# A norm between two projections, cut into halves of the tokens and put between the products of its neighbours

## The reference

```python
    y = merged @ w_out[l]
    x = x + gate * _rms(y, g_post[l])
...
    hn = rms_norm(h, norm_mixer[i])        # h is that x
...
    proj = h @ w_in                        # q, k, v, g, a_lr of the GLA mixer
    log_a = log_sigmoid(a_lr @ w_a2 + b_a) / 16
```

## Time and profile before

| | |
|---|---|
| median of three runs | 2327.85 us |
| the profiled execution | 2328.21 us |
| its span, first to last instruction | 2326.0 us |
| TensorE busy | 2200.5 us (95%) |
| VectorE busy | 1205.2 us (52%) |
| ScalarE busy | 856.5 us (37%) |
| GpSimd busy | 554.3 us (24%) |
| TensorE's mean granted clock | 0.975 |

### The profile page before, as it was taken

How to read it: one execution, slowest core, us unless ns; L and a number is a source line. 1 busy time by engine, 2 the same in 40 slices (tenths; PEclk the granted TensorE clock), 3 DMA queues, 4 the chain that set the end, 5 groups by cost and what they waited for, 6 DMA issues and landing times.

```text
span 2326.0 us, 29165 instructions
## 1 busy us (share of the span) xinstructions
PE 2200.5 (95%) x11168; PEld 1853.8 (80%) x11168; DVE 1205.2 (52%) x1488; ACT 856.5 (37%) x1295; POOL 554.3 (24%) x292
## 2 busy tenths in 40 slices
PE   4999999999999699999899979999999999999996
PEld 4778888988887598898778868888888888877885
DVE  6963332543331724334345454566666667676744
ACT  3136653112021323323322123446546546544311
POOL 1322221333333122222233222211111111111520
PEclk9999999999999699999999989999999999999998
DMA  8112222112331211101131121111111011012201
GB/s 338 53 46 73 73 72 73 55 37 89 137 136 46 82 36 46 37 28 46 36 138 44 46 99 56 37 46 36 45 54 43 29 54 45 27 45 101 81 19 73
DMA packets 36660, 154.59 MB, mean 66 GB/s; under 512 B 4161, under 2 KB 4161, under 8 KB 35810
## 3 DMA queue, kind: packets, MB, share of 16 engines
q1 hardware_dynamic: 23840, 93.52, 11.6%
q10 hardware_dynamic: 12738, 59.87, 7.2%
HBM read 128.15 MB, written 21.04 MB: 64 GB/s over the span
## 4 chain that ended last, share of the span: by engine, by line
PE 83%; DVE 11%; issue 4%; ACT 2%; DMA 0%; DVEq 0%; SPq 0%; ACTq 0%
PE psG L311 21%; PE psG L312 21%; PE psG L313 21%; PE psA L311 3%; PE psA L313 2%; PE psA L312 2%; PE psA L1884 1%; PE psA L1883 1%; PE psA L1858 1%; PE psA L1784 1%; DVE M L871 1%; PE psA L399 1%; DVE AL L824 1%; DVE AL L849 1%; PE psA L1867 1%
## 5 line engine op out<-in xcount | busy, mean ns | idle before, releaser
L311 PE MATMUL psG<-AH,WH 128*128 128x512 f32 x2108 | 856.8, 406 | 40.3 <-DVE AL L849 15.3
L312 PE MATMUL psG<-AL,WH 128*128 128x512 f32 x2108 | 831.8, 395 | 0.0
L313 PE MATMUL psG<-AH,WL 128*128 128x512 f32 x2108 | 830.8, 394 | 0.0
L298 POOL TENSOR_SCALAR WH<-RAW 128x1024 fp32r<-128x1024 f32 x144 | 165.3, 1148 | 1685.3 <-PE psG L311 1195.7
L311 PEld LDWEIGHTS psG<-AH,WH 128*128 128x128 f32 x2108 | 401.7, 191 | 124.7 <-issue 28.0
L313 PEld LDWEIGHTS psG<-AH,WL 128*128 128x128 f32 x2108 | 401.3, 190 | 88.1
L312 PEld LDWEIGHTS psG<-AL,WH 128*128 128x128 f32 x2108 | 402.9, 191 | 69.5
L300 POOL TENSOR_TENSOR WL<-RAW,WH 128x1024 fp32r<-128x1024 f32 x144 | 389.2, 2703 | 12.0
L2183 DVE TENSOR_TENSOR FTL<-PF,FTH 128x512 fp32r<-128x512 f32 x192 | 112.8, 588 | 129.2 <-ACT FTH L2058 127.2
L2051 ACT ACTIVATE PF<-psA,PB 128x512 f32<-128x512 f32 x192 | 111.3, 580 | 91.6 <-PE psA L1886 52.1
L2193 DVE RECIPROCAL FDR<-psA 64x128 f32<-64x128 f32 x128 | 118.2, 939 | 32.1 <-PE psA L313 30.5
(11 more groups left out here) (331 smaller groups left out, 2961.3 us busy)
## 6 DMA issues: line engine op xcount, KB each, us to landing
RAW<-w_tiles SPq DMA_DIRECT2D x144, 512.0 KB, 3.5
gates<-SIG ACTq DMA_DIRECT2D x16, 512.0 KB, 2.9
park<-X ACTq DMA_DIRECT2D x2, 4096.0 KB, 11.1
CB<-fox_c ACTq DMA_DIRECT2D x16, 512.0 KB, 4.3
X<-xT SPq DMA_DIRECT2D x4, 1024.0 KB, 11.9
WADA_SCALE<-w_ada SPq DMA_DIRECT2D x1, 4096.0 KB, 24.0
WADA_SHIFT<-w_ada SPq DMA_DIRECT2D x1, 4096.0 KB, 34.0
WADA_GATE<-w_ada ACTq DMA_DIRECT2D x1, 4096.0 KB, 16.4
```

The costliest lines, as they stand in the source:

```text
L298: nc.gpsimd.tensor_scalar(WH[:, i, :], RAW[:, i % RAW_SLOTS, :], 1.0, 0.0, ALU.mult, ALU.add).then_inc(w_high, 1)
L311: first = nc.tensor.matmul(out, wh, xh, start=start, stop=False)
L312: nc.tensor.matmul(out, wh, xl, start=False, stop=False)
L313: return first, nc.tensor.matmul(out, wl, xh, start=False, stop=stop)
```

## The change

**Output projection of block 1** (`pe_block1_out`). Tiles 0 to 3 are computed as before. Tiles 4 to 7 are computed first for the low 512 tokens (LO), into the four banks of `psG`, then for the high 512 (HI) into the same banks. Between the slices of the HI products TensorE does the half sum and half spread of the first norm, and eight half sums of the squares of the updated x, one for each chunk, into columns of their own of `psA`, which VectorE adds up (`tensor_reduce`). VectorE updates x for LO in this time, with PSUM banks 1 and 3 of `psA` for its products.

**The next tiles** (`pe_gla_begin`). LR and q are computed for LO, chunk by chunk, q two chunks behind LR; between them the sum and spread of the first norm for HI. Then k for LO with a half sum of the HI squares behind each of its eight slices; the spread; LR and q for HI; the logits of head 0; k for HI. The cumulated decay follows behind k now, where it stood before k. k goes to `psA` and q and the logits change units (`gla_buf`).

ScalarE's and VectorE's lists follow with twice as many instructions of 512 columns; the parking of x (a DMA of 4 MB) is issued behind the HI updates.

**Weighted sums** (`weigh`). Of the three matmuls of a piece the one with `FTL` is now the third and only it waits for `ft_ready`; the first two wait for `ft_high`.

```diff
+    def pe_block1_out(pe):
+        for j in range(WHOLE):
+            gemm(pe, T_WO + j, U_WO + j, (T_WO + j) % 4, (U_WO + j) % 2, fill=2 if j == 0 else None)
+        for j in range(WHOLE, KC):
+            pe.wait_ge(w_split, T_WO + j + 1)
...
+            for c in range(KC):
+                f, l = half_cut(psG[:, j - WHOLE, :], (T_WO + j) % 4, c, LO)
...
+            l.then_inc(wo_full, 1)
+        for j in range(WHOLE, KC):
+            pe.wait_ge(wo_free, j - WHOLE + 1)
+            for c in range(KC):
+                f, l = half_cut(psG[:, j - WHOLE, :], (T_WO + j) % 4, c, HI)
+                if j > WHOLE and c == 0:
+                    f.then_inc(tile_begun, 1)
+                if (j, c) == (WHOLE, 2):
+                    pe.wait_ge(lo_added, KC - WHOLE)
+                    pe_half_sums(RS, 0, 0)[1].then_inc(lo_sums, 1)
+                elif (j, c) == (WHOLE, 4):
+                    pe.wait_ge(lo_rec, 1)
+                    pe_half_spread(0).then_inc(lo_spread, 1)
+                elif (j - WHOLE) * KC + c in LO_SUMS_AT:
+                    pe_lo_squares(LO_SUMS_AT.index((j - WHOLE) * KC + c))
+            l.then_inc(psum_full, 1)
+        pe.wait_ge(lo_rec, 2)
+        pe_half_spread(0).then_inc(lo_spread, 1)
+
+    def pe_gla_begin(pe):
+
+        lag, q = 2, T_GLA % 4
+        for n in range(KC + lag):
+            if n < KC:
...
+                pe.wait_ge(lo_ready, n + 1)
+                f, l = half_cut(psG[:, 0, :], T_LR % 4, n, LO)
...
+            if n >= lag:
...
+                half_cut(psG[:, 2, :], q, n - lag, LO)
+            if n == 0:
+                pe.wait_ge(sq_used, sq_base(2))
+                pe_half_sums(RS, 1, 8)[1].then_inc(sum_full, 1)
+            elif n == 3:
+                pe.wait_ge(rc_ready, 2)
+                pe_half_spread(1).then_inc(rs_full, 1)
+        pe.wait_ge(w_split, T_GLA + 2)
+        for j in range(KC):
+            half_cut(psA[:, 3, :], (T_GLA + 1) % 4, j, LO)
+            pe.wait_ge(sq_ready, KC * SPLIT_NORM + j + 1)
+            third, l = pe_half_sums(SQ[:, j % 2, :], 1, 16 + 4 * j)
...
+        pe.wait_ge(rc_ready, 3)
+        pe_half_spread(1).then_inc(rs_full, 1)
+        for n in range(KC + lag):
+            if n < KC:
+                pe.wait_ge(a_ready, KC * 3 + n + 1)
+                _, l = half_cut(psG[:, 1, :], T_LR % 4, n, HI)
...
+            if n >= lag:
+                f, l = half_cut(psG[:, 3, :], q, n - lag, HI)
...
+        pe.wait_ge(wa_loaded, 32)
+        pe.wait_ge(psum_free, U_LR + 1)
+        pe_gla_logits(pe, 0)
+        for c in range(KC):
+            f, l = half_cut(psA[:, 2, :], (T_GLA + 1) % 4, c, HI)
...
     def dve_block1_out(dve):
...
+        def update(j, cols, spread, done):
+
+            if j >= 2:
+                dve.wait_ge(done, j - 1)
+
+            rows_ = psA[:, 1 + 2 * (j % 2), :] if cols == LO else TN[:, j % 2, cols]
+            link(nc.vector.scalar_tensor_tensor(rows_, Y[:, j, cols], GG[:, j:j + 1], spread, ALU.mult, ALU.mult))
+            nc.vector.tensor_tensor(X[:, j, cols], X[:, j, cols], rows_, ALU.add).then_inc(done, 1)
...
+        for j in range(KC + 1):
+            fill(j, LO, lo, (0, 0), lo_tn, lo_high, lo_ready)
+            if j == 2:
+                dve.wait_ge(rms_ready, 2)
+                nc.vector.reciprocal(RC[:, 4:8], RC[:, 4:8]).then_inc(rc_ready, 1)
         dve.wait_ge(rs_full, 2)
         for j in range(KC):
...
+            update(j, HI, hi, x_upd)
+        dve_gla_in(dve)
+        dve.wait_ge(sum_full, 3)
...
             r, h, n, lo, w = piece(j)
-            pe.wait_ge(ft_ready, p * N_P + (j + 1))
+            pe.wait_ge(ft_high, p * N_P + (j + 1))
...
             vs = slice(HD * r, HD * r + P)
-            _, l = three(psA[:, 2 + r, HALF - w:HALF], FVH[:, n, vs], FVL[:, n, vs], FTH[:, j % 2, 0:w], FTL[:, j % 2, 0:w],
-                         n == 0, j in ENDS)
-            l.then_inc(fpv_done, 1)
+            out = psA[:, 2 + r, HALF - w:HALF]
+            nc.tensor.matmul(out, FVH[:, n, vs], FTH[:, j % 2, 0:w], start=n == 0, stop=False)
+            nc.tensor.matmul(out, FVL[:, n, vs], FTH[:, j % 2, 0:w], start=False, stop=False)
+            pe.wait_ge(ft_ready, p * N_P + (j + 1))
+            nc.tensor.matmul(out, FVH[:, n, vs], FTL[:, j % 2, 0:w], start=False, stop=j in ENDS).then_inc(fpv_done, 1)
```

More of the change, by code:

```diff
@@ L400, in pe_sums, with pe_half_sums @@
         return l
[L402 to L408, removed]
+    LO, HI = slice(0, HALF), slice(HALF, S)
+    WHOLE = KC // 2
+    def pe_half_sums(src, h, at):
+        for n in range(NB // 2):
+            s = (NB // 2 * h + n) * P
+            l = nc.tensor.matmul(psA[:, 2, at + n:at + n + 1], src[:, s:s + P], mat("ones")[:, 0:1], start=True, stop=True)
+            if n < NB // 2 - 1:
+                third = l
+        return third, l
@@ new lines, in build, with pe_lo_squares, pe_half_spread, half_cut @@
+    LO_SUMS_AT = [12, 14, 17, 19, 22, 24, 27, 29]
+    def pe_lo_squares(j):
+        pe = nc.tensor
+        pe.wait_ge(lo_squares, KC - WHOLE + j + 1)
+        pe_half_sums(SQL[:, j % 2, :], 0, 48 + 4 * j)[1].then_inc(lo_taken, 1)
+    def pe_half_spread(h):
+        for n in range(NB // 2):
+            m = NB // 2 * h + n
+            l = nc.tensor.transpose(psA[:, h, n * P:(n + 1) * P], RC[:, m:m + 1].to_broadcast([P, P]), mat("ident"))
+        return l
+    def half_cut(out, slot, c, cols):
+        ws = slice(c * P, (c + 1) * P)
+        return three(out, WH[:, slot, ws], WL[:, slot, ws], AH[:, c, cols], AL[:, c, cols], c == 0, c == KC - 1)
@@ new lines, in copy_hi, with fill_lo @@
+        def copy_hi(j):
+            nc.scalar.activation(Y[:, j, HI], psG[:, j - WHOLE, :], ACT.Copy).then_inc(psum_free, 1)
+        behind = {0: 4, 2: 5, 5: 6}
+        for j in range(KC):
+            updated(j)
+            if j in behind:
+                square_hi(behind[j])
+                copy_hi(behind[j])
+        square_hi(KC - 1)
+        act.wait_ge(sum_added, 1)
+        act_half_root(0, RC[:, 0:4]).then_inc(lo_root, 1)
+        copy_hi(KC - 1)
+        def fill_lo(j):
+            act.wait_ge(lo_tn, j + 1)
+            nc.scalar.activation(AH[:, j, LO], TN[:, j % 2, LO], ACT.Copy).then_inc(lo_high, 1)
@@ L775, in build @@
+        for j in range(KC):
+            act.wait_ge(tn_ready, KC + j + 1)
+            nc.scalar.activation(AH[:, j, HI], TN[:, j % 2, HI], ACT.Copy).then_inc(a_high, 1)
     chain = Chain(nc.vector, dve_step)
@@ new lines, in fill, with low @@
+        def fill(j, cols, spread, base, tn, high, ready):
+            def low(j):
+                dve.wait_ge(high, base[1] + j + 1)
+                nc.vector.tensor_tensor(AL[:, j, cols], TN[:, j % 2, cols], AH[:, j, cols].bitcast(F32), ALU.subtract).then_inc(ready, 1)
+            if j < KC:
+                if j >= 2:
+                    dve.wait_ge(ready, base[1] + j - 1)
+                nc.vector.scalar_tensor_tensor(TN[:, j % 2, cols], X[:, j, cols], col("norm0", j), spread, ALU.mult, ALU.mult).then_inc(tn, 1)
+            if j:
+                dve.wait_ge(tn, base[0] + j)
+                low(j - 1)
@@ new lines, in dve_block1_out @@
+        for j in range(1, WHOLE):
+            dve_square(dve, 1, j)
+        for j in range(WHOLE, KC):
+            add_lo(j)
+        dve.wait_ge(lo_root, 1)
+        nc.vector.reciprocal(RC[:, 0:4], RC[:, 0:4]).then_inc(lo_rec, 1)
+        dve.wait_ge(lo_spread, 1)
+        dve.wait_ge(x_loaded, 16)
+        behind = {1: 4, 4: 5, 6: 6}
+        for j in range(KC):
+            update(j, LO, lo, lo_upd)
+            if j in behind:
+                add_hi(behind[j])
+        dve.wait_ge(lo_taken, KC)
```

203 lines of the change are left out of this document (129 added, 74 removed).

## The result

The changed kernel takes 2300.6 us (median of four runs, 2299.2 to 2300.9) against 2327.9 (four runs, 2324.4 to 2328.4): a ratio of 0.988 with a 95% interval of 0.9868 to 0.9892. The profiled executions, span against span, differ by 27.0 (2326.0 to 2299.0).

What follows compares the result with a forecast made beforehand. TensorE was taken as busy almost throughout, losing time to waits and half clock in the middle stage. Gains of 14.0 there and 4.2 in the weighted sums, 18.2 us, took 2327.85 to 2309.6, stated as 2310, range 2303 to 2321.

Steps and rivals of the forecast that it cites:

- The weighted sums: Fox stage, 192 pieces: FTL product third and alone waiting for FTL gains 4.2 us, bounds 0 and 4.9.
- the rival that they give nothing: Weighted sums in the fox stage: another wait takes the place, so no gain there and 2314 us; chance 0.08.
- Items 1 to 6 of the middle stage: From the projection's HI products, ending at 757.8, to LR and q on HI, ending at 810.1 us.
- Turns between slices and sums: Middle stage: at the far bound, 16 turns cost 0.3 us more each and take off 4.8.
- The rival of item 4: k on LO: clock falls, 1.44 us more a turn, 8.6 for six turns; 2318, late fall 2313; chance 0.33.
- The rule of the Trainium skill about brief idle spots: Brief idle spots between product groups can make the clock oscillate; HI products and k on LO would then slow.
- items 1 and 4: HI products with sums between slices, ending 757.8; k on LO with eight HI sums, 13.0 us, to 792.9.
- items 3 and 6: LR and q on LO, to 779.9, and on HI, to 810.1; each starts at low clock.
- The low bound of the range: 2303 us: the middle stage without its low clock, short of the full gain of 23.
- Item 7: Logits, k on HI, cumulated decay: new wait of some 2 us for LAH; value tokens effectively at 822.6.

Runs made afterwards that it cites:

- the three traces with the same code: Changed kernel with weighted sums undone, with their new order alone, or with one product ahead of the FTL wait: 2310.9, 2310.9 and 2301.9 us.

## Why the prediction was wrong, and where it was right

- **The weighted sums** are the step that failed: a term of 4.2 us with an upper bound of 4.9, which measured 9.4 by the marks and 10.3 by the medians with the edit undone. The mechanism was right (two products ahead of the wait cover it, the wait inside the piece is free, the slots don't open up), and the rival that they give nothing was wrong. The size and its bound were read from the waits view as if the 4.9 us were all that could be won. That view counts only what is left behind the drawn end of a product, 0.17 after its slot; it leaves out what is late by less, and the 0.1 at the restart. Undoing the edit (10 us), doing it alone (9), the order alone (0) and one product of cover (four fifths) settle it. With 9.4 in the place of 4.2 the forecast would have been 2304.8, inside the range; the last 4 us are those below.
- **Items 1 to 6 of the middle stage** held to 0.8 us at each mark, partly because small errors cancel. A half spread costs 0.35 us of TensorE between products and not 1.0, taken from a bound that held VectorE's handover too; that is 0.65 for each that stands between products. A slice at the low clock is 1.28, as charged, which is 1.9 times the 0.68 and not twice. Against that, a step of fill is 1.39 and not 1.32, and an AL was held by GpSimd for 0.8 (0.3 in the three traces with the same code), which nothing in the prediction has. The half sum at 0.95 was right: it moves the next product by 0.81 and that one the next by 0.1.
- **Turns between slices and sums,** charged with 0.3 at the far bound, cost nothing. **The rival of item 4** had the right mechanism and the wrong dose, as the run with doubled sums shows: at one sum a slice it came in no trace, at two it did. The rule of the Trainium skill about brief idle spots was set against items 1 and 4. Nothing there agrees with it, with 25 and 12.7 us at 1.00, but TensorE was idle for only 0.75 and 0.0 us of them, so they hardly try it.
- **The clock in items 3 and 6** fell where the prediction has it, priced at 3.3 and 2.4. In the HI turn VectorE's fill sets the pace and the low clock was almost hidden behind it: from the spread to the logits it is 15.6 us with none of it and with 3.4 us of it, 16.1 with 6.8. In the LO turn it does cost: with the last 3.4 us of it gone, k on LO starts 1.6 earlier. The low bound of the range counted both as gains at the full price.
- **Item 7**: LAH ended at 818.85 and the new wait is 1.7, as forecast. The further 1.5 for a low clock on the first value products didn't come; clock 1.00 from 800 on. This and item 6, which took 12.7 and not 13.3, make the stage 15.9 and not 14.0. The three traces with the same code have 1.0 to 1.2 more.
- **The stage of the heads**, 1.8 us from value tokens to PH, was not in the sum. Before has 355.8 us there, the changed kernel 354.0, and its variants 350.8 to 355.8 with the same code there, with the short stretches at 0.50 in different places. So the 1.8 is no gain of the change that could be shown; what made it in this execution stays open.

From 2310: 5.2 for the weighted sums, 1.9 for the stage and 1.8 for the heads make 2301.1, against 2300.6 measured. The first is a mis-sized term, most of the second a cost that was charged and didn't come, and the third is luck as far as the traces tell.

## What to carry to other kernels

The gain of hiding a short, frequent wait is read from the starts of the instructions, as the start to start of the pair that spans the wait less its slot, over all the places and not only those that a view of waits lists; here it was twice the wait. Sums with a one-column product cost little between products of 512 columns as long as they are few, and the dose is worth a run of its own, since doubling them behind the slices of k brought 38 us at half clock. Where two engines take turns at a fill, look at what a third one running beside them does to the length of their instructions before its work is called hidden. And before a gain of a microsecond at a mark is believed, look at what the same code does at that mark in another execution: here it was 1.2.

## What the runs showed of the hardware

- A product of 512 columns has a slot of 0.23 us and is drawn 0.39 to 0.40 long; behind the stalls shown above the product after the late one starts 0.10 to 0.11 late too.
- One half sum (eight products 128x1) behind each slice of three products left the clock at 1.00 for all of 12.7 us; with two behind each it was 0.50 for 37.6 us, of which TensorE was busy 34.5.
- With GpSimd cutting a weight tile, a VectorE subtraction with both inputs in SBUF took 0.96 to 2.34 instead of 0.69 in eight traces, and ended 0.54 to 0.55 behind GpSimd's instruction in each; GpSimd's copy took 1.18 to 1.48. With the cut elsewhere the subtraction took 0.68 to 0.69 in three traces, the copy 1.04 to 1.05 in two and 1.22 in the third.
- A half spread of four transposes takes 0.60 to 0.65, and moves the next product by 0.35 at full clock (730.93 to 731.28).
